# Layer 1's cross-attention with the second query slab made beside its first units

## What is computed

```
proj = h @ w_in
q, k, v, f_logit, xq = split(proj)          # q, k, v: 8 heads of 64; xq: 4 heads of 128
q = rms_norm(q.reshape(B, S, 8, 64), q_gain)
k = rms_norm(k.reshape(B, S, 8, 64), k_gain)
...
s = einsum("bhqd,bhkd->bhqk", q, k) / 8 + c_q - c_k    # forgetting attention, causal
o = softmax(s) @ v
...
s = einsum("bshd,bmhd->bhsm", rms_norm(xq), k_mem) / sqrt(128)   # cross-attention
p = softmax(s)
o_mem = einsum("bhsm,bmhd->bshd", p, v_mem)
x = x + concatenate([o, o_mem]) @ w_out
```

## Time and profile before

| | us |
|---|---|
| median of 3 runs | 2770.85 (2769.64 to 2772.02) |
| profiled execution | 2767.77 |
| its span | 2766.0 |
| TensorE busy in the span | 2714.1 |
| VectorE busy | 1585.2 |
| ScalarE busy | 993.4 |

### The profile page before, as it was taken

One profiled execution on the slowest core, in us unless ns is written; L12 is line 12 of the kernel. 1 busy time (PEld: TensorE's weight loads), 2 busy tenths in 40 slices (PEclk: granted clock), 3 DMA queues, 4 the chain that ended last, 5 costly groups with the idle time before them and its releaser, 6 DMA issues.

```text
span 2766.0 us, 45708 instructions
## 1 busy us (share of the span) xinstructions
PE 2714.1 (98%) x19386; PEld 2257.4 (82%) x19386; DVE 1585.2 (57%) x2327; ACT 993.4 (36%) x1372; POOL 187.7 (7%) x272
## 2 busy tenths in 40 slices
PE   9999999999899999999999999999999999999999
PEld 7878888899688888877878888888878878888887
DVE  5668777864667777765563553333585454633334
ACT  5643212344632222363332432223453333422223
POOL 4000000000000000001050000000010220000000
PEclk9999999999999999999999999999999999999999
DMA  4333655522045555330023223222210123232231
GB/s 159 107 113 123 186 163 177 165 77 77 1 134 181 169 169 166 100 100 19 4 81 105 94 92 107 92 94 90 76 60 19 33 92 107 77 105 94 94 100 65
DMA packets 239934, 281.19 MB, mean 102 GB/s; under 512 B 9718, under 2 KB 227330, under 8 KB 239746
## 3 DMA queue, kind: packets, MB, share of 16 engines
q1 hardware_dynamic: 226426, 226.29, 25.6%
q0 software_dynamic: 13184, 52.11, 6.4%
q10 hardware_dynamic: 136, 0.03, 0.0%
HBM read 276.31 MB, written 2.10 MB: 101 GB/s over the span
## 4 chain that ended last, share of the span: by engine, by line
PE 89%; DVE 5%; ACT 3%; issue 2%; POOL 1%; DMA 0%; DVEq 0%; SPq 0%; ACTq 0%; POOLq 0%
PE psum L2603 25%; PE psum L2605 24%; PE psum L2604 24%; DVE wlo L1684 1%; PE psum L2684 1%; PE psum L2685 1%; PE psum L2686 1%; PE psum L3215 1%; PE psum L3200 1%; PE psum L3183 1%; ACT whi L945 1%; PE psum L3239 1%; PE psum L2618 1%; POOL mo L884 0%; PE psum L3172 0%
## 5 line engine op out<-in xcount | busy, mean ns | idle before, releaser
L2603 PE MATMUL psum<-hh,whi 128*128 128x512 f32 (+1 forms) x2016 | 780.9, 387 | 5.2 <-DVE wlo L1684 4.4
L2605 PE MATMUL psum<-hh,wlo 128*128 128x512 f32 (+1 forms) x2016 | 771.6, 383 | 0.0
L2604 PE MATMUL psum<-hl,whi 128*128 128x512 f32 (+1 forms) x2016 | 771.5, 383 | 0.0
L1684 DVE TENSOR_TENSOR wlo<-raw,whi 128x2048 fp32r<-128x2048 f32 x217 | 498.9, 2299 | 459.7 <-ACT whi L945 459.5
L945 ACT ACTIVATE whi<-raw 128x2048 fp32r<-128x2048 f32 x217 | 414.4, 1910 | 520.9 <-PE psum L2605 516.8
L2603 PE MATMUL psum<-mh,whi 128*128 128x512 f32 (+1 forms) x1248 | 485.9, 389 | 1.3 <-issue 1.0
L2604 PE MATMUL psum<-ml,whi 128*128 128x512 f32 (+1 forms) x1248 | 479.7, 384 | 0.0
L2605 PE MATMUL psum<-mh,wlo 128*128 128x512 f32 (+1 forms) x1248 | 479.7, 384 | 0.0
L2603 PEld LDWEIGHTS psum<-hh,whi 128*128 128x128 f32 x2016 | 379.1, 188 | 92.0 <-issue 9.1
L2605 PEld LDWEIGHTS psum<-hh,wlo 128*128 128x128 f32 x2016 | 379.1, 188 | 74.1
L2604 PEld LDWEIGHTS psum<-hl,whi 128*128 128x128 f32 x2016 | 379.4, 188 | 72.5 <-issue 0.5
(11 more groups left out here) (483 smaller groups left out, 2780.9 us busy)
## 6 DMA issues: line engine op xcount, KB each, us to landing
rest<-in_ada_w POOLq DMA_DIRECT2D x64, 768.0 KB, 5.3
raw<-in_w_gu SPq DMA_DIRECT2D x44, 1024.0 KB, 5.1
raw<-in_w_in SPq DMA_DIRECT2D x34, 1024.0 KB, 5.2
raw<-in_w_mlp_in SPq DMA_DIRECT2D x32, 1024.0 KB, 5.4
raw<-in_w_mlp_out SPq DMA_DIRECT2D x32, 1024.0 KB, 5.2
raw<-in_w_out SPq DMA_DIRECT2D x16, 1024.0 KB, 5.1
raw<-in_w_down SPq DMA_DIRECT2D x16, 1024.0 KB, 4.9
raw<-in_w_mem_kv SPq DMA_DIRECT2D x8, 1024.0 KB, 5.1
```

The costliest lines, as they stand in the source:

```text
L1684: ins = dve.tensor_tensor(wlo[:, g % 2, :, :], raw[:, g % 2, :, :], f32(whi[:, g % 2, :, :]), ALU.subtract)
L2603: pe.matmul(out, whi_, xhi, start=first, stop=False)
L2604: pe.matmul(out, whi_, xlo, start=False, stop=False)
L2605: return pe.matmul(out, wlo_, xhi, start=False, stop=last)
```

## The change

In layer 1 the four tiles of q's second slab are no longer made ahead of the cross-attention; tile i is made in step i of its loop, for i from 0 to 3, by `fill`, on TensorE behind the step's scores and transposes and ahead of its values, on ScalarE and VectorE at the end of the step. As in `token_heads`, the root and the product of tile b stand one step behind its square. The queries are turned at step 5 instead of step 2, and the jobs of the plan follow. The roots of this slab are taken as Exp(0.5 x Ln(x)) instead of Sqrt(x), two activations of which the second waits for the first. Since `hh` and `hl` are now read during the cross-attention, layer 1's `a_p` and `a_t` move into `mo` and `rest`. The 20 unread products of layer 1 are left out. Layer 0 keeps all it has.

```diff
+TURN_Q = 5
@@ Plan.attend
             if layer == 0 and i < units:
                 self.block(("memk", "memv")[i // 4], 1, i // 2 % 2, i % 2)
+            if layer and i < NT:
+                self.block("q", 1, 1, i)
             if i >= VALUES:
                 self.add(name + "_o", layer, i - VALUES)
-            if layer and i == 2:
+            if layer and i == TURN_Q:
                 for t in range(4):
                     self.add("qT", t)
@@ Plan.walk
                 self.add("xs", 1)
-                self.slab_jobs("q", 1, 1, NT)
@@ program
-        a_p = carve(ho, 2 * B, RING, T)
-        a_t = carve(ho, 2 * B + RING * T, RING, T)
+        a_p = [[carve(buf, at + i * T, T) for i in range(RING)] for buf, at in ((ho, 2 * B), (mo, 0))]
+        a_t = [[carve(ho, 2 * B + (RING + i) * T, T) for i in range(RING)],
+               [carve(mo, RING * T, T), carve(rest, B + T, T), carve(rest, B + 3 * T, T)]]
@@ scalar
-                    if between and i == 2:
+                    if between and i == TURN_Q:
                         between()
...
-                    def token_heads(name, s, x):
+                    def token_heads(name, s, x, tiles=range(NT + 1)):
 
-                        for b in range(NT + 1):
+                        for b in tiles:
...
                                 act.wait_ge(S("head_sum"), n + 1)
-                                act.activation(hn[:, 0, c:c + 4], hn[:, 0, c:c + 4], ACT.Sqrt, scale=1.0 / HD,
-                                               bias=tk[:, 2, b - 1:b]).then_inc(S("head_root"), 1)
+                                if (name, s) == ("q", 1):
+                                    q.step(act.activation(hn[:, 0, c:c + 4], hn[:, 0, c:c + 4], ACT.Ln, scale=1.0 / HD,
+                                                          bias=tk[:, 2, b - 1:b]))
+                                    act.activation(hn[:, 0, c:c + 4], hn[:, 0, c:c + 4], ACT.Exp, scale=0.5)\
+                                       .then_inc(S("head_root"), 1)
+                                else:
+                                    act.activation(hn[:, 0, c:c + 4], hn[:, 0, c:c + 4], ACT.Sqrt, scale=1.0 / HD,
+                                                   bias=tk[:, 2, b - 1:b]).then_inc(S("head_root"), 1)
...
                     hi(slab_of("wo", 0))
-                    token_heads("q", 1, 3)
+
+                    def query_tiles(i):
+
+                        if i <= NT:
+                            token_heads("q", 1, 3, (i,))
...
-                          (lambda: turned("qT", qh, gq8[:, 0:1])) if l else None, None if l else beside_units)
+                          (lambda: turned("qT", qh, gq8[:, 0:1])) if l else None, query_tiles if l else beside_units)
@@ vector: between at TURN_Q, token_heads with tiles, and
                     lo(slab_of("wo", 0))
-                    token_heads("q", 1, 3, qn)
+
+                    def query_tiles(i):
+
+                        if i <= NT:
+                            token_heads("q", 1, 3, qn, (i,))
@@ tensor
-                        if u == 0:
-                            idle_products(20 if l else 6, name + "_t", l, u)
+                        if u == 0 and l == 0:
+                            idle_products(6, name + "_t", l, u)
...
-                    linear_tokens("q", l, 1, h, NT)
...
+                    def query_tiles(i):
+
+                        if i < NT:
+                            linear_tokens("q", l, 1, h, NT, only=i)
...
                 attention("xa", l, 2 * XA_H, 8 * l, xa_scores, xa_turn, xa_values,
-                          (lambda: turned("qT", qn, "q")) if l else None, None if l else memory_beside)
+                          (lambda: turned("qT", qn, "q")) if l else None, query_tiles if l else memory_beside)
```

More of the change, by code:

```diff
@@ L1038, in attention @@
                         n = cols(u)
-                        free(act.activation(a_t[:, u % RING, 0:n], bank(j)[:, 0:n], ACT.Copy), j)
+                        free(act.activation(a_t[l][u % RING][:, 0:n], bank(j)[:, 0:n], ACT.Copy), j)
                     u = i - STORE
@@ L1302, in xa_parts @@
                     c = 2 * XA_H * (i % 2) + i // 2
-                    return [(a_p[:, i % RING, s * MEM:(s + 1) * MEM], b[:, s * MEM:(s + 1) * MEM],
+                    return [(a_p[l][i % RING][:, s * MEM:(s + 1) * MEM], b[:, s * MEM:(s + 1) * MEM],
                              xr[:, 1, c + XA_H * s:c + XA_H * s + 1]) for s in range(2)]
@@ L1809, in attention @@
                         for s in range(parts):
-                            x = a_p[:, (i - 1) % RING, s * n:(s + 1) * n]
+                            x = a_p[l][(i - 1) % RING][:, s * n:(s + 1) * n]
                             ins = dve.tensor_scalar(x, x, stat[:, 2, c + s:c + s + 1], None, ALU.mult)
@@ L2017, in _, with token_heads @@
                 else:
-                    def token_heads(name, s, x, dst):
-                        for b in range(NT + 1):
+                    def token_heads(name, s, x, dst, tiles=range(NT + 1)):
+                        for b in tiles:
                             if b < NT:
@@ L2120, in _ @@
                 attention("xa", l, 2 * XA_H, 8 * l, lambda i: (2, MEM), xa_factor, xa_o,
-                          (lambda: turned("qT", 4, qh, ql, gq8[:, 0:1])) if l else None, None if l else beside_units)
+                          (lambda: turned("qT", 4, qh, ql, gq8[:, 0:1])) if l else None, query_tiles if l else beside_units)
                 if l:
@@ L3022, in xa_turn @@
                             ins = pe.transpose(p[:, k * MEM + s * P:k * MEM + (s + 1) * P],
-                                               a_p[:, i % RING, s * MEM + k * P:s * MEM + (k + 1) * P], ident[:, :])
+                                               a_p[l][i % RING][:, s * MEM + k * P:s * MEM + (k + 1) * P], ident[:, :])
                     return ins
@@ L3028, in xa_values @@
                         ins = pe.matmul(p[:, 0:MEM], mV[l][:, k, (i // 2) * P:(i // 2 + 1) * P],
-                                        a_t[:, i % RING, k * MEM:(k + 1) * MEM], start=(k == 0), stop=(k == MT_ - 1))
+                                        a_t[l][i % RING][:, k * MEM:(k + 1) * MEM], start=(k == 0), stop=(k == MT_ - 1))
                     return ins
                 attention("xa", l, 2 * XA_H, 8 * l, xa_scores, xa_turn, xa_values,
-                          (lambda: turned("qT", qn, "q")) if l else None, None if l else memory_beside)
+                          (lambda: turned("qT", qn, "q")) if l else None, query_tiles if l else memory_beside)
                 if l:
```

## The result

| | before | after |
|---|---|---|
| median, us | 2770.24 (6 runs) | 2782.60 (6 runs) |
| ratio | | 1.0051, 95% interval 1.0041 to 1.0061 |
| profiled execution, its span | 2767.77, 2766.0 | 2787.17, 2785.2 |
| ahead of the first score product of unit 0 | 665.93 | 667.37 |
| from there to the first product of the forgetting attention ("the stage") | 41.49 | 53.82 |

The medians differ by 12.4 us. Before, the stage counts from 665.93, the place where the prediction puts unit 0's scores (four tiles ahead of the first score product), so that both columns hold the same work. The stage is 12.33 us longer. The profiled execution after the change is the slowest of its six. The 1.4 us ahead of the stage and the 5.5 behind it lie in code whose text the change doesn't touch.

The account below looks back on a forecast made before the run. TensorE, busy 98% of the span, was taken as the bound, the stage's idle time set by a ScalarE-VectorE round. Stage +11.4 us (10.3 from eight loads) plus 0.5 for the clock gave 2770.85 + 11.9 = 2782.7; range 2779 to 2787.

Parts of the forecast that it names:

- R0: VectorE's first reduction (R0 to R7: one per unit of layer 1's cross-attention) at 671.73 instead of 679.49, 7.8 us earlier.
- R7: VectorE's reduction for unit 7 in layer 1's cross-attention: at 712.3, 1.2 us later than a round of 3.26.
- Second slab beside the units: Query tiles move behind scores of units 0 to 3; first reduction, held by VectorE's slab split, comes 7.8 us earlier.
- Eight loads: Likeliest case: each root's logarithm and the exponential behind it load a table set on ScalarE, 10.3 us; chance 0.86.
- the list: Signs of being right: nine table loads between 672 and 702 instead of one, eight at the root's two activations.
- The upper bound: A root on ScalarE takes 2 x (1.29 + 0.34) = 3.26 us, as logarithm and following exponential each load a set.
- The new bank wait: TensorE stands 4 us ahead of unit 7's scores, whose PSUM bank VectorE frees with output 2's low part.
- Clock falls: TensorE's gaps in the stage lower its granted clock, slowing products: +0.5 us taken, bounds nothing and +2.6.
- Unread products: Layer 1's 4.46 us of unread TensorE products go, hidden before; TensorE idles in their place, losing their clock cover.
- Buffers, and all behind the stage: Moved buffers cost nothing; everything after the stage moves as a block, clock falls there 1 us either way.
- Rival (1): Roots use the set with both functions: +1.1, up to 1.3 and 1.5 more, 2771.9 to 2775; chance 0.09.
- Rival (2): TensorE bounds the cross-attention, ScalarE and VectorE inside its 5.05 round: 2760, or 2765.4 for half; chance 0.03.

Follow-up runs that it names:

- e9: e4's kernel with the split of the output projection's first slab moved from ahead of the cross-attention to its step 9; 2774.00 us, ratio 1.0022 to the kernel before.
- e2: Changed kernel with the set holding Exp and Ln named by one load ahead of the waits before unit 0's exponentials; 2769.79 us, ratio 1.0012 to the kernel before.
- e1: Changed kernel with the set holding Exp and Ln named by one load at unit 0's exponentials, behind the waits; 2773.28 us, ratio 1.0023 to the kernel before.
- e7: Changed kernel with 14 unread products put ahead of unit 0's transposes in layer 1; 2781.87 us, ratio 1.0048 to the kernel before.
- e6: Kernel before without layer 1's 20 unread products, nothing else changed; 2770.19 us, ratio 1.0007 to the kernel before.
- e4: e2's kernel with the queries turned at step 8 instead of 5; 2768.73 us, ratio 1.0006 to the kernel before.
- e5: e4's kernel plus 8 unread products ahead of unit 0's transposes; 2769.87 us, ratio 1.0008 to the kernel before.
- e12: e4's kernel with the split of the output projection's first slab moved behind step 9 of the forgetting attention; 2769.47 us, ratio 1.0003 to the kernel before.
- e10: e4's kernel unchanged, a second profile and second set of runs; 2770.88 us, ratio 1.0010 to the kernel before.
- e3: Changed kernel with Sqrt again for the second slab's roots instead of Exp of half of Ln; 2777.85 us, ratio 1.0037 to the kernel before.

## Why the prediction was right

The forecast was 2782.7, the measured median 2782.6, in the likeliest case (eight table loads). Its steps, counted from unit 0's first score product:

| step | predicted | measured |
|---|---|---|
| first reduction (R0) | 5.80 | 5.88 |
| R1 | 9.9 | 9.98 |
| R2 | 16.0 | 16.08 |
| R4 | 29.2 | 29.26 |
| R5 | 35.8 | 35.85 |
| R6 | 41.9 | 41.98 |
| R7 | 46.4 | 47.30 |
| end of the stage | 52.9, and 0.5 for the clock | 53.82 |

- **Second slab beside the units:** R0 stood behind the slab split, as said. e9 shows it: with the split elsewhere unit 0's exponentials come 3.48 us earlier (3.37 instead of 6.85). That is more than VectorE's 2.29, since VectorE also waits 1.33 for ScalarE's rounding there (the row at 671.04), and e9 moved both.
- **Eight loads:** all nine loads of the list are there, and the root took 3.26 (679.36 + 0.28 = 679.64, the square's turn, to the reciprocal at 682.90). The upper bound was right because of how sets are chosen, which e1 shows directly. The price of the loads was put at 10.3 us, in the rounds only. e2's 12.9 are 1.3 of unit 0's load, 10.8 in the rounds and 0.8 at unit 7's scores. e1 leaves the first load in place and gains 8.9, with the same 10.8 and 0.8 in it: the two rounds that its low clock made longer, which long rounds had hidden, take 2.7 of it back.
- **The skill's rules:** e1 agrees with the Trainium skill's ScalarE: Activation LUTs, section "Table sets: the hidden batching unit": one set does hold Exp and Ln, and then the pair needs no second load. The longest run of ScalarE activation tables: per-element evaluation and per-set limits, section "Table sets in the compiler and the runtime", is not what happened: that set serves the whole run from 675.50 on, and eight loads were placed. (The page says it of each block of the program; no row shows where a block would end.) Of the drain of 1.38 us in "What ACT_TABLE_LOAD costs" no row shows anything: the logarithm at 681.05 starts 0.01 behind its load's end (679.76 + 1.28), and the second load 0.02 behind the logarithm.
- **The new bank wait:** forecast as 4 us, ended by the low part, and found as 2.15 ended by the low part (L1831). It is shorter only because TensorE, at half clock, came later itself (in e2, at full clock, it is 3.69). Its end, 45.37, is 0.1 from the forecast's.
- **Clock falls:** this term was a little too small. +0.5 was taken, of bounds 0 and 2.6. The end is 0.95 later than the sum without it: 0.08 is there from R0 on, and 0.87 in one row, unit 7's scores, which took 1.89 instead of 1.02. Of that the clock has 0.74, as e7 shows, where the same scores behind their wait took 1.13 at full clock and the stage was 0.74 shorter. That a fall counts only at unit 7's scores was right, though the clock was at 0.50 for some 20 us of the stage (a mean of 0.81 over 53.82).
- **Unread products:** nothing, and e6, e7 agree.
- **Buffers, and all behind the stage:** put at nothing, 1 us either way, and no run shows that. The rest was 5.5 us longer in the profile after, and longer in all eight profiles of the new order than in any of the old one. Whether buffers or order do it is open.
- **Slips:** R7 is 711.2 + 1.02 = 712.2, not 712.3, and the lower end of the range adds up to 2779.6, not 2779. Neither changes anything.
- **The end:** the stage is right to 0.5 us, and step by step, so the mechanism is. That the median came out 0.1 from the forecast is luck: the profiled execution itself was 7.5 above its forecast 2779.7, most of it outside the stage (1.4 ahead, 5.5 behind), and in e7, which differs by 14 unread products, the distance to the kernel before was 13.6, not 12.4.

Rival (1), the shared set loaded at unit 0's exponentials, is what e1 builds. Its price of +1.1 with at most 2.8 more holds the stage, 3.4 longer than before, but not the median, whose ratio of 1.0023 is +4 to +9 us. It had the clock falls on the tail; in e1 the one that cost lay at query tile 2. Rival (2) needed ScalarE and VectorE inside TensorE's round of 5.05. They were (3.88 without loads), and of the obstacles it named e9 removes R0's wait for the slab split and e4 the bank of unit 7's scores. With both gone TensorE is the bound in the first 21.7 us, and the scores of units 2, 3 and 4 start 4.18 and 5.05 apart, the rounds that the rival named. Behind the tiles it waits again, and the stage fell to 36.5, against 30.6 if all idle time had gone. No version beat the kernel before: e5 and e12 are level with it within their intervals, and e4's kernel in one set of runs, not in the other (e10).

## What to carry to other kernels

Before functions are mixed on ScalarE, look in the trace at where loads stand, name the set that holds them all, and put that load into ScalarE's idle time ahead of a wait: here one line was worth 12.9 us of the stage. If two sets can't be avoided, place the switch so that what the other engine waits for comes ahead of the second load, not behind it. And follow a moved piece of VectorE's work into the next stage before counting its gain: here waits of 2 to 3 us that it made there cost themselves and the slow products behind them.

## What the runs showed of the hardware

- A table load stands ahead of the wait of its activation: in e3 it ran for 1.28 us of the time in which ScalarE waited anyway, so a round with two loads took 5.07 there and 6.58 where both loads came ahead of what VectorE waited for (0.2 of the difference is one more activation).
- The placement of loads did not see the shared set until it was named; after that it left every Exp, Ln and Copy of the stage alone.
- How long TensorE waited did not settle what its clock did. Behind most waits of 2.1 us or more shown here it went to its lower level, and stayed there for some 14 us in the stage after the change, some 10 in e9 and e12, some 7 in e1; behind e3's wait of 3.05 us and e7's of 2.52 it stayed at full speed. Behind waits of 1.3 to 1.4 it differed from one profile of the same kernel to the next (45.8 and 48.7 us for the same forgetting attention).
- A low clock cost only where TensorE was on the path: nothing in e6, 0.74 us in the stage after the change though the clock was low for some 20, and 2.7 in e1.
